# Filter spectra of a hybrid SSD and Hyena layer: eight tap groups in a row, then eight groups of the second transform, in place of two and two in turn

## The reference, cut to what matters

```python
filt = (hid @ w_out).reshape(seqlen, 2, H_ORDER, H_WIDTH)
window = jnp.exp(-t[:, :, None, None] * deltas)
filt = filt * window
...
k = jnp.concatenate([h_fwd[:1] + h_bwd[:1], h_fwd[1:], zeros, jnp.flip(h_bwd[1:], axis=0)])
k_f = jnp.fft.rfft(k, n=2 * seqlen, axis=0)
```

## Time and profile before

| what | value |
|---|---|
| time before, median of 3 executions | 3490.57 us (3483.76 to 3492.51) |
| time of the profiled execution | 3485.99 us |
| its span, first to last instruction | 3484.2 us |
| mean granted TensorE clock | 0.964 |
| TensorE matmul busy | 3254.0 us (93% of the span) |
| weight loads busy | 2652.2 us (76%) |
| VectorE busy | 2019.9 us (58%) |
| ScalarE busy | 1434.3 us (41%) |
| GpSimd busy | 1934.5 us (56%) |

### The profile page before, as it was taken

How to read it: one execution, slowest core, us unless ns; L and a number is a source line. 1 busy time by engine, 2 the same in 40 slices (tenths; PEclk the granted TensorE clock), 3 DMA queues, 4 the chain that set the end, 5 groups by cost and what they waited for, 6 DMA issues and landing times. The chain is left out here.

```text
span 3484.2 us, 68175 instructions
## 1 busy us (share of the span) xinstructions
PE 3254.0 (93%) x28310; PEld 2652.2 (76%) x28310; DVE 2019.9 (58%) x2365; ACT 1434.3 (41%) x2699; POOL 1934.5 (56%) x1326
## 2 busy tenths in 40 slices
PE   7899999999699999997899989999779997999997
PEld 3677888888488888886899966767567886788886
DVE  6697887222896885222353345555466775767662
ACT  5433222333433223334365445555457763333332
POOL 0486999777787998773000025243467653444442
PEclk9999999999799999998799999999989998999998
DMA  8444333323243333232423564654675655655552
GB/s 301 154 147 149 114 105 119 115 109 109 103 145 123 107 118 118 103 115 91 119 100 116 182 175 131 169 153 120 223 299 167 200 176 189 221 201 190 191 188 97
DMA packets 390043, 527.19 MB, mean 151 GB/s; under 512 B 152685, under 2 KB 269189, under 8 KB 388743
## 3 DMA queue, kind: packets, MB, share of 16 engines
q1 hardware_dynamic: 316913, 398.56, 36.0%
q10 hardware_dynamic: 72824, 124.27, 9.4%
HBM read 351.51 MB, written 171.25 MB: 150 GB/s over the span
## 5 line engine op out<-in xcount | busy, mean ns | idle before, releaser
L765 PE MATMUL pl_bank<-hl_hi,pl_a_hi 128*128 128x512 f32 x2056 | 814.2, 396 | 40.8 <-DVE hl_lo L397 28.2
L767 PE MATMUL pl_bank<-hl_hi,pl_a_lo 128*128 128x512 f32 x2056 | 805.6, 392 | 0.0
L766 PE MATMUL pl_bank<-hl_lo,pl_a_hi 128*128 128x512 f32 x2056 | 805.1, 392 | 0.0
L710 POOL TENSOR_TENSOR pl_a_lo<-hl_early_x,pl_a_hi 128x512 fp32r<-128x512 f32 x288 | 433.8, 1518 | 117.5 <-ACT pl_a_hi L814 117.2
L765 PEld LDWEIGHTS pl_bank<-hl_hi,pl_a_hi 128*128 128x128 f32 x2056 | 388.7, 189 | 128.6 <-DVE hl_lo L397 28.1
L767 PEld LDWEIGHTS pl_bank<-hl_hi,pl_a_lo 128*128 128x128 f32 x2056 | 388.9, 189 | 82.5
L766 PEld LDWEIGHTS pl_bank<-hl_lo,pl_a_hi 128*128 128x128 f32 x2056 | 389.3, 189 | 78.3
L814 ACT ACTIVATE pl_a_hi<-hl_early_x 128x512 fp32r<-128x512 f32 x288 | 181.8, 633 | 540.6 <-PE pl_bank L767 449.2
L2315 POOL TENSOR_TENSOR mo_w_lo<-mo_w,mo_w_hi 128x1024 fp32r<-128x1024 f32 x96 | 239.4, 2496 | 278.0 <-ACT mo_w_hi L2386 278.0
L710 POOL TENSOR_TENSOR pl_a_lo<-hl_w,pl_a_hi 128x512 fp32r<-128x512 f32 x220 | 312.6, 1434 | 113.1 <-ACT pl_a_hi L814 113.0
L2343 PE MATMUL mo_bank<-mo_hi,mo_w_hi 128*128 128x512 f32 x768 | 305.2, 397 | 21.6 <-POOL mo_w_lo L2315 17.0
(11 more groups left out here) (237 smaller groups left out, 6032.5 us busy)
## 6 DMA issues: line engine op xcount, KB each, us to landing
hl_w<-in_w_rec SPq DMA_DIRECT2D x146, 512.0 KB, 3.3
mo_w<-in_w_br SPq DMA_DIRECT2D x96, 512.0 KB, 3.6
spec_s<-filt_res SPq DMA_DIRECT2D x64, 512.0 KB, 3.4
tab_win<-spec_s SPq DMA_DIRECT2D x240, 128.0 KB, 2.8
g_s<-pl_res ACTq DMA_DIRECT2D x32, 512.0 KB, 2.6
conv_gin<-u_s SPq DMA_DIRECT2D x32, 512.0 KB, 4.1
st_s<-st_state ACTq DMA_DIRECT2D x32, 512.0 KB, 3.5
y_st<-st_s SPq DMA_DIRECT2D x16, 1024.0 KB, 8.8
```

The source lines that it names most:

```text
L710: nc.gpsimd.tensor_tensor(a_lo[:, at % NS, :], src, a_hi[:, at % NS, :].bitcast(F32), ALU.subtract).then_inc(s_lo, 1)
L765: pe.matmul(out, a_hi[:, q, m], op_hi[:, b, k, :], start=begin, stop=False)
L766: pe.matmul(out, a_hi[:, q, m], op_lo[:, b, k, :], start=False, stop=False)
L767: return pe.matmul(out, a_lo[:, q, m], op_hi[:, b, k, :], start=False, stop=end)
```

## The change

On TensorE, in each item but the last, all eight tap groups of the next item are issued in a row behind `first`, and then all eight groups of the second transform; before, two and two took turns. `sums` in item 3 stays between the fourth and the fifth second group.

On ScalarE the four decays of odd items move: they stood behind the copies of groups 0 to 3 and now stand ahead of the first copy, since TensorE now reaches the second groups only when all tap groups have been issued, and the last tap groups wait for these windows by way of VectorE. The decays of even items stay where they were. VectorE's, GpSimd's and SyncE's programs are the same as before.

```diff
                 if i == 0:
                     turned()
-                for g in range(0, NGR, 2):
+                for m in range(NGR):
                     if i + 1 < NI:
-                        taps(i + 1, g)
-                        taps(i + 1, g + 1)
+                        taps(i + 1, m)
+                for g in range(NGR):
                     if i == 3 and g == 4:
                         sums()
                     second(i, g)
-                    second(i, g + 1)
...
                     nc.scalar.activation(sp_w, e, ACT.Ln, bias=1.0).then_inc(s_act, 1)
+                if o == 1 and b + 1 < NBK:
+                    for m in range(4, NGR):
+                        decay(b + 1, m)
                 for g in range(NGR):
...
                     if b + 1 < NBK:
                         if o == 0 and 2 <= g < 6:
                             decay(b + 1, g - 2)
-                        if o == 1 and g < 4:
-                            decay(b + 1, g + 4)
```

## The result

The changed kernel takes 3528.1 us at the median of four executions (3527.4 to 3529.6), the kernel before 3488.7 beside it: 1.0114 times as long, 95% interval 1.0102 to 1.0126, 39.4 us slower. The forecast was 28.4 slower: the direction was right, the size too small by 11. By the profiled executions (3527.43 against 3485.99) the loss is 41.4, and 40.4 of it lie in the seven stages, 218.4 us against 178.0.

What follows compares the result with a forecast made beforehand. The prediction took TensorE's own instructions and switches to bound each stage, other engines hiding. Terms 8.4 + 11.7 + 7.7 - 1.4 + 2 = 28.4 us slower gave 3519 us at the median; range 3500 to 3548.

Steps and rivals of the forecast that it cites:

- What bounds a stage, and that both covers go: Stages: TensorE's instructions and switches set the length; alternation hides VectorE and ScalarE, and the change ends both covers.
- A plain stage loses 1.2, seven times 8.4: Each of seven stages: taps take 10.5 us instead of 7.84, stage 25.0 against 23.8; 8.4 us lost, bounds 6.5 to 9.5.
- TensorE needs 0.98, so it waits: Tap row: TensorE needs 0.98 us a group, VectorE's emptying of two buffers allows one per 1.30, so TensorE waits.
- instructions arrive late: Rival, chance 0.10: rows of many short tap instructions wait for instructions; 17 us more, 3536, or 3565 at 6.6 each.
- ScalarE 11.7: Items 0, 2, 4: copy plus decay, 3.24 us, hold up second groups; 3.9 us lost, three times.
- Chores 7.7 and clock 2: Items 1 and 2: VectorE's step chores among tap multiplies cost 7.7 us; the clock falling after TensorE's standstills costs 2.
- Sums 1.4 gained: Item 3: with no decay ahead on ScalarE, the sums of the steps hold TensorE 3.3 us instead of 4.7.
- Item 5 between -2.5 and +3: Item 5: the step table's write falls among the second groups; taken as nothing, between 2.5 us gained and 3 lost.
- the likeliest case: The forecast itself, chance 0.66: 28.4 us slower, 3519 us at the median, bounds 3510 to 3527.
- the clock's fall in the even items: Rival, chance 0.12: `first` after even items runs at half clock, 12.3 us a time; 3531 for one, 3556 for three.
- only the eviction pace: Rival, chance 0.08: decays and chores find cover, only the 8.4 us of VectorE's emptying pace is left; 3499.
- the switches: Rival, chance 0.04: VectorE keeps nearer TensorE's pace, seven stages save 1.3 us each and item 5's pauses go; 3479.

Runs made afterwards that it cites:

- e1: Changed kernel with the four decays of even items also moved ahead of ScalarE's copies; median 3517.2 us, ratio 1.0071 to the kernel before.
- e3: Changed kernel with half of the tap matmuls and weight loads left out from the second item on; one execution, 3517.4 us.
- e4: Changed kernel with one of the two VectorE multiplies of each tap group left out from the second item on; one execution, 3527.2 us.
- e6: Kernel before with one tap group and one second group in turn instead of two and two; ratio 1.0016 to the kernel before.
- e2: Changed kernel with VectorE's step work moved behind the eighth tap multiply of its stage; median 3522.9 us, ratio 1.0090 to the kernel before.

## Why the prediction was right, and where its size was off

- *What bounds a stage, and that both covers go*: right for ScalarE (e1), half right for VectorE. e3 has VectorE's pace bare (10.1 us for the row, 10.5 forecast, with a first group half as long), but by e4 that pace isn't what binds the row of the changed kernel: the instructions are. The multiplies do not stand in unbroken rows 1.30 apart, as the prediction's signs had it.
- *A plain stage loses 1.2, seven times 8.4*: the term that was mis-sized. It measured 3.8, seven times 26.7, far outside its bounds of 6.5 to 9.5. The step that failed is "TensorE needs 0.98, so it waits": TensorE needs 0.98 only while its instructions are there. With VectorE's waits 256 instructions last 2.6 us, and in these rows they come every 3.5 at best. e3 (fewer instructions), e4 (less VectorE) and e6 (instructions spread out) agree.
- The second rival, *instructions arrive late*, is what came, on top of the forecast as it had it. Its price was near by luck (2.5 us a stage, taken from item 5's crowded transfers, against 2.6), and its argument against was wrong: "when the DMA engines have nothing to do" doesn't help, since the three pauses of item 6 fall where the transfers are idle but for the instructions. The Trainium skill, "Runtime: NRT & Kernel Launch", section "Instruction fetch mechanics", gives blocks of 256 instructions, and the 128 matmuls and 128 weight loads between pauses agree; that they are hidden by issue does not hold here.
- The sign stood in the stage that the prediction called the cleanest. Of the 1.47 us that it took for the price of the switches, 0.54 were such a pause:

```profile
1956.92 0.18 PEld L1162 LDWEIGHTS filt_front<-filt_w,filt_hid 64*32 64x32 f32 x14 [0.54 <-issue]
```

- *ScalarE 11.7*: right. The second groups of items 0, 2 and 4 last 18.4 us each against 14.5, the 3.9 forecast; e1 gave 10.6 back over the whole stages.
- *Chores 7.7 and clock 2*: 4.9 by e2 together, 4.3 after the 0.6 that before had lost there. "All of it counts" was wrong: while TensorE waits for VectorE, the next portion comes in, so the chores' time and the pauses overlap. In item 2, behind a wait of 4.05 us, no pause put to "issue" is left among the taps. The clock did fall in both items.
- *Sums 1.4 gained*: they took from 1866.8 to 1870.1, the 3.3 forecast; item 3's stage, +1.6 in all against +3.8 for a plain one, gained 2.2.
- *Item 5 between -2.5 and +3*: +1.0, through ScalarE's wait of 4.26 us for a store and the clock's fall behind it.

26.7 + 10.6 + 4.3 - 2.2 + 1.0 = 40.4, the stages' difference; the last two terms are what their stages left over. That the total came so near is in part luck: the plain stages cost 18.3 us more than forecast, all other terms together 6.3 less. The result is 1 us above the likeliest case's own bounds and lies inside the range because that reached up for another rival, the clock's fall in the even items, which didn't come about: `first` of item 1 ran at a granted 1.00, and so for items 3 and 5 (1831 to 1846 and 1924 to 1939, 15.2 us each). The other two rivals, only the eviction pace and the switches, would both have come out faster than the forecast.

Open stays why a portion takes 3.5 to 4.0 us when transfers are idle, and why e4's came later than the changed kernel's. A packet moves 2.2 to 2.9 us before each pause ends; whether it is the portion that is waited for, or the next, no run here shows.

## What to carry to other kernels

Letting two kinds of work take turns on one engine is worth more than the switches cost when each kind's partner engine is slower than the engine itself: the turn is the partner's cover, and small chores and in-order queues hide under it too. Here it also spread the short tap instructions over time. Before many small matmuls are put in a row, count the instructions per microsecond and look whether pauses put to "issue" come at equal instruction counts; a prologue that already runs in that order, as here, shows both its pace and its pauses, though there among crowded transfers.

## What the runs showed of the hardware that I had not expected

With the DMA engines idle but for the instructions, TensorE went on after each pause of a tap row only 3.5 to 4.0 us after the pause before, that is 256 instructions later (128 weight loads and 128 matmuls of 64x32 tiles). `first`, whose 256 last 7.6 us, ran without such a pause in all items behind the prologue. TensorE at 1.81 us of work in every 3.24 over four groups kept 2.4 GHz in items 0, 2 and 4 (granted 1.00), while stops of 3 to 4 us in items 1 and 2 were followed by 1.2 GHz (0.75 and 0.66 on average over 5 us).
